# Modulation products in four column groups of TensorE, and another order of the attention units

## What is computed

```python
def trunk_layer(x, mod, lp, rope, ctx_kv):
    sh1, sc1, g1, sh2, sc2, g2 = jnp.split(mod, 6, axis=-1)   # mod = silu(c) @ w_mod + b_mod
    h = layer_norm(x) * (1.0 + sc1) + sh1
    mix, own_kv = token_mixer(h, lp, rope, ctx_kv)
    ...

def diff_attention(q, k, v, lam):          # 4 heads, two maps of 64 each, values of 128
    s = jnp.einsum('bqhmd,bkhmd->bhmqk', qb, k) * scale
    a = jax.nn.softmax(s, axis=-1)
    w = a[:, :, 0] - lam * a[:, :, 1]
    return jnp.einsum('bhqk,bkhd->bqhd', w, v)

def gqa_attention(q, k, v):                # 8 heads of 64, taken two at a time
    s = jnp.einsum('bqhgd,bkhd->bhgqk', qb, k) * scale
    return jnp.einsum('bhgqk,bkhd->bqhgd', jax.nn.softmax(s, axis=-1), v)
```

## Time and profile before

| what | value |
|---|---|
| median of 3 runs | 5316.12 us (5314.84 to 5319.43) |
| the profiled execution | 5326.6 us, its span 5324.8 us |
| mean granted clock of TensorE | 0.898 of full speed |
| PE busy | 4320.0 us, 81% of the span |
| DVE busy | 3689.9 us, 69% |
| ACT, POOL busy | 1406.7 us (26%), 2141.4 us (40%) |

### The profile page before, as it was taken

How to read it: one execution, slowest core, us unless ns; L and a number is a source line. 1 busy time by engine, 2 the same in 40 slices (tenths; PEclk the granted TensorE clock), 3 DMA queues, 4 the chain that set the end, 5 groups by cost and what they waited for, 6 DMA issues and landing times.

```text
span 5324.8 us, 65913 instructions
## 1 busy us (share of the span) xinstructions
PE 4320.0 (81%) x23486; PEld 3688.6 (69%) x23486; DVE 3689.9 (69%) x5666; ACT 1406.7 (26%) x1999; POOL 2141.4 (40%) x1267
## 2 busy tenths in 40 slices
PE   7988799714479999999889888997144799999996
PEld 5855688513369888988778556894133798889885
DVE  2323323689979999999951333236999799999998
ACT  3233311111133332332232332112011333233331
POOL 2200000003368877887621000000133687778874
PEclk9988899857689999999999789998576899999998
DMA  4111111202279999999831211111022899999996
GB/s 169 69 48 66 64 72 72 72 16 71 63 262 404 394 368 366 401 400 362 326 130 55 79 63 52 72 72 71 0 81 85 305 406 385 365 377 402 394 367 241
DMA packets 326651, 1074.16 MB, mean 202 GB/s; under 512 B 25344, under 2 KB 123696, under 8 KB 275824
## 3 DMA queue, kind: packets, MB, share of 16 engines
q0 software_dynamic: 151168, 552.73, 27.3%
q1 hardware_dynamic: 75536, 464.03, 22.4%
q10 hardware_dynamic: 99808, 55.58, 3.6%
HBM read 1012.72 MB, written 59.51 MB: 201 GB/s over the span
## 4 chain that ended last, share of the span: by engine, by line
PE 36%; DVE 31%; POOL 11%; issue 9%; DVEq 8%; ACT 3%; DMA 2%; ACTq 0%; SPq 0%; POOLq 0%
PE PS L547 13%; POOL got L522 10%; DVE acc L1745 9%; PE PS L556 6%; PE PS L557 6%; PE PS L558 6%; DVEq L1746 5%; DVE ring_lo L1719 5%; DVE ohE L1694 3%; PE PS L551 2%; DVE ohA L1694 1%; DVE wtmp L1726 1%; ACT hT L987 1%; DVE got L1742 1%; ACT prob L1110 1%
## 5 line engine op out<-in xcount | busy, mean ns | idle before, releaser
L522 POOL DMA_INDIRECT got<-v_rows,sidx x512 | 878.6, 1716 | 281.4 <-DVE acc L1745 187.8
L522 POOL DMA_INDIRECT got<-u_rows,sidx x512 | 889.0, 1736 | 223.1 <-issue 144.3
L503 POOL TENSOR_TENSOR ohB<-ohE,idxT 128x512 f32<-128x512 f32 x192 | 254.1, 1323 | 1571.8 <-DVE ohE L1694 1571.8
L1265 ACT CAST ring_hi<-ring 128x2048 fp32r<-128x2048 f32 x256 | 489.2, 1912 | 1237.4 <-DMA ring<-weights 1237.4
L556 PE MATMUL PS<-hT_hi,ring_hi 128*128 128x384 f32 x2048 | 688.1, 336 | 55.2 <-DVE ring_lo L1719 55.2
L558 PE MATMUL PS<-hT_hi,ring_lo 128*128 128x384 f32 x2048 | 687.9, 336 | 0.0
L557 PE MATMUL PS<-hT_lo,ring_hi 128*128 128x384 f32 x2048 | 687.2, 336 | 0.0
L556 PE MATMUL PS<-ring_hi,W_hi 128*128 128x512 f32 x1536 | 611.3, 398 | 90.5 <-DVE W_lo L1732 90.5
L1745 DVE SCALAR_TENSOR_TENSOR acc<-got,weight,acc 128x1024 f32<-128x1024 f32 x512 | 657.9, 1285 | 37.1 <-issue 13.2
L1742 DVE SCALAR_TENSOR_TENSOR got<-got,hT 128x1024 f32<-128x1024 f32 x512 | 604.7, 1221 | 27.9 <-issue 16.7
L1719 DVE TENSOR_TENSOR ring_lo<-ring,ring_hi 128x2048 fp32r<-128x2048 f32 x256 | 586.5, 2292 | 29.8 <-issue 29.5
(11 more groups left out here) (251 smaller groups left out, 7912.2 us busy)
## 6 DMA issues: line engine op xcount, KB each, us to landing
ring<-weights SPq DMA_DIRECT2D x392, 1024.0 KB, 7.7
gate_matrix<-stg ACTq DMA_DIRECT2D x12, 4096.0 KB, 15.9
G<-gate_matrix SPq DMA_DIRECT2D x128, 384.0 KB, 9.4
got<-u_rows,sidx POOLq DMA_INDIRECT x512, 8.9
got<-v_rows,sidx POOLq DMA_INDIRECT x512, 8.3
x_wait<-x POOLq DMA_DIRECT2D x2, 2560.0 KB, 24.5
x_mix<-x_wait ACTq DMA_DIRECT2D x2, 2560.0 KB, 9.5
lnr<-lnrows POOLq DMA_DIRECT2D x4, 1024.0 KB, 5.0
```

Source lines behind the costliest of these rows:

```text
L503: nc.gpsimd.tensor_tensor(ohB[:, u % 2, :, :], ohE[:, u % 2, :, :], g, ALU.mult).then_inc(oh_ready, 1)
L522: pool.indirect_dma_start(out=got[:, n % GB, :], out_offset=None, in_=u_rows[:, :] if phase % 2 == 0 else v_rows[:, :], in_offset=bass.Ind ...
L1265: nc.scalar.copy(ring_hi[:, s, :], ring[:, s, :]).then_inc(hi_ready, 1)
```

## The change

Three edits:

1. `cnds` is padded to 32 columns (30 of them zero, by a memset on DVE and a new semaphore `cond_clear`). Product c of a slot goes to column group c % 4 of the array, and its result to PSUM rows 32(c % 4) to 32(c % 4)+31, so a group adds up two products, not eight. The four partial sums are added in `mod_columns`, whose contraction is now over all 128 rows, with a 0/1 selector (`C_SEL`, two more columns of `const`) in place of the identity. ACT's copies to `mrow` have 128 rows, not 2.
2. In attention PE issues scores two units ahead (behind the modulation, scores(1), and then scores(u+2) in unit u: ahead of the transposes for u < 4, behind values(u-1) for u = 4 and 5). ACT runs exps(u+1) ahead of probs_out(u). DVE runs maxima(u+1) ahead of weights_of(u).
3. To make room, the fifth transposed piece of map 0 moves from the unit's own score bank to bank 7, beside the results of values. ACT copies the fifth piece first, and values(u-1) on PE waits for the fifth piece of unit u (`fifth_ready`), since it writes the same bank.

```diff
-        cnds, o = at("cnds", [KC, 2], o)
+        cnds, o = at("cnds", [KC, 32], o)
...
-            return (bank(6), bank(b, 0, P)) if m == 0 else (bank(b + 2), bank(b + 1, 0, P))
+            return (bank(6), bank(7, 0, P)) if m == 0 else (bank(b + 2), bank(b + 1, 0, P))
...
-                    group(out, [(cnds[:, c, :], w[:, c, :]) for c in range(KC)]).then_inc(mod_full, 1)
+                    for c in range(KC):
+                        g = c % 4
+                        last = mm(out[32 * g:32 * g + 32, :], cnds[:, c, :], w[:, c, :], start=(c < 4), stop=(c >= 4))
+                    last.then_inc(mod_full, 1)
...
-                        last = mm(out[:, 2 * k:2 * k + 2], mrow[0:2, k * P:k * P + P], ident[0:2, 0:2],
+                        last = mm(out[:, 2 * k:2 * k + 2], mrow[:, k * P:k * P + P], const[:, C_SEL:C_SEL + 2],
...
-                    modulation(MOD1 + k, PS[0:2, 256 * k:256 * k + 256])
+                    modulation(MOD1 + k, PS[:, 256 * k:256 * k + 256])
...
                             pe.wait_ge(p_ready, base + u - 1)
-                            pe.wait_ge(pT_ready, base_t + turn_group(u - 2, 0 if u < 6 else 1) + 1)
+                            if u >= 6:
+                                pe.wait_ge(pT_ready, base_t + turn_group(u - 2, 1) + 1)
...
                             pe.wait_ge(o_ready, base + u)
+                        if nk == 5:
+                            pe.wait_ge(fifth_ready, (l * (NT - 1) + t - 1) * UNITS + min(u + 2, UNITS))
...
+                    scores(1)
                     for u in range(UNITS):
-                        if u + 1 < UNITS:
-                            scores(u + 1)
+                        if u < 4:
+                            scores(u + 2)
                         for m in range(1 if u < 4 else 2):
                             turn_probs(u, m)
                         if u >= 1:
                             values(u - 1)
+                        if 4 <= u < UNITS - 2:
+                            scores(u + 2)
                     values(UNITS - 1)
...
-                            nc.scalar.copy(pT[:, u % 2, m, 0:4, :].rearrange("p k n -> p (k n)"), four)
-                            nc.scalar.copy(pT[:, u % 2, m, 4, :], fifth).then_inc(pT_ready, 1)
+                            last = nc.scalar.copy(pT[:, u % 2, m, 4, :], fifth)
+                            if m == 0:
+                                last.then_inc(fifth_ready, 1)
+                            nc.scalar.copy(pT[:, u % 2, m, 0:4, :].rearrange("p k n -> p (k n)"), four).then_inc(pT_ready, 1)
...
                     for u in range(UNITS):
+                        if u + 1 < UNITS:
+                            exps(u + 1)
                         for m in range(1 if u < 4 else 2):
                             probs_out(u, m)
-                        if u + 1 < UNITS:
-                            exps(u + 1)
...
                     for u in range(UNITS):
-                        weights_of(u)
                         if u + 1 < UNITS:
                             maxima(u + 1)
+                        weights_of(u)
                         if u >= 1:
                             outputs(u - 1)
```

More of the change, by code:

```diff
@@ L96 @@
 N_GATHER = PHASES * P
-C_ID, C_IOTA, C_COS, C_SIN, C_NSIN, C_ROPEC, C_ROPES, C_ONE, C_LAM, C_BASE = 0, 128, 256, 384, 512, 640, 768, 896, 1024, 1028
-NCONST = 1030
+C_ID, C_IOTA, C_COS, C_SIN, C_NSIN, C_ROPEC, C_ROPES, C_ONE, C_LAM, C_BASE, C_SEL = 0, 128, 256, 384, 512, 640, 768, 896, 1024, 1028, 1030
+NCONST = 1032
 def layer_at(l, per_layer, n):
@@ L193, in trunk @@
         mtmp, t = at("mtmp", [T], t)
-        otmp, t = at("otmp", [2, 256], t)
         oall, _ = at("oall", [NT, D], z_at)
@@ L200, in trunk @@
         lnr, t = at("lnr", [2, D], t)
+        otmp, t = at("otmp", [2, 256], t)
         assert t <= f_at
@@ L275, in trunk @@
         kv_stored = sem("kv_stored")
+        cond_clear = sem("cond_clear")
         cond_ready = sem("cond_ready")
@@ L306, in trunk @@
         t_full = sem("t_full")
+        fifth_ready = sem("fifth_ready")
         pT_ready = sem("pT_ready")
@@ L747, in attend @@
                         for k in range(4):
-                            modulation(MOD2 + k, PS[0:2, 1536 + 256 * k:1792 + 256 * k], t - 1)
+                            modulation(MOD2 + k, PS[:, 1536 + 256 * k:1792 + 256 * k], t - 1)
                         mod_columns(l * N_COL + t + 2, bank(6, 0, 16))
+                    scores(1)
                     for u in range(UNITS):
-                        if u + 1 < UNITS:
-                            scores(u + 1)
+                        if u < 4:
+                            scores(u + 2)
                         for m in range(1 if u < 4 else 2):
@@ L967, in _ @@
             act.wait_ge(setup, 48)
-            A(cnds[:, :, :], cnd[:, :, :], ACT.Silu).then_inc(cond_ready, 1)
+            act.wait_ge(cond_clear, 1)
+            A(cnds[:, :, 0:2], cnd[:, :, :], ACT.Silu).then_inc(cond_ready, 1)
             used = lamw[:, 11:12]
@@ L995, in mod_rows @@
                         act.wait_ge(col_full, n)
-                    nc.scalar.copy(mrow[0:2, :], src).then_inc(mrow_ready, 1)
+                    nc.scalar.copy(mrow[:, :], src).then_inc(mrow_ready, 1)
                 for n in range(2):
-                    mod_rows(layer_at(l, N_MOD, 4 * n + 4), layer_at(l, N_COL, n) if n else None, PS[0:2, 1024 * n:1024 * n + 1024])
+                    mod_rows(layer_at(l, N_MOD, 4 * n + 4), layer_at(l, N_COL, n) if n else None, PS[:, 1024 * n:1024 * n + 1024])
                 root(0, NT)
@@ L1121, in probs_out @@
                         else:
-                            nc.scalar.copy(pT[:, u % 2, m, 0:4, :].rearrange("p k n -> p (k n)"), four)
-                            nc.scalar.copy(pT[:, u % 2, m, 4, :], fifth).then_inc(pT_ready, 1)
+                            last = nc.scalar.copy(pT[:, u % 2, m, 4, :], fifth)
+                            if m == 0:
+                                last.then_inc(fifth_ready, 1)
+                            nc.scalar.copy(pT[:, u % 2, m, 0:4, :].rearrange("p k n -> p (k n)"), four).then_inc(pT_ready, 1)
                     exps(0)
                     if nk == 5:
-                        mod_rows(l * N_MOD + 8 + t * 4, l * N_COL + t + 1, PS[0:2, 1536:2560])
+                        mod_rows(l * N_MOD + 8 + t * 4, l * N_COL + t + 1, PS[:, 1536:2560])
                     for u in range(UNITS):
+                        if u + 1 < UNITS:
+                            exps(u + 1)
                         for m in range(1 if u < 4 else 2):
                             probs_out(u, m)
-                        if u + 1 < UNITS:
-                            exps(u + 1)
                     act.wait_ge(o_full, base + UNITS)
@@ L1320, in _ @@
             reduce = nc.vector.tensor_reduce
+            nc.vector.memset(cnds[:, :, :], 0.0).then_inc(cond_clear, 1)
             dve.wait_ge(setup, 48)
@@ L1835, in constants @@
     base = [layer * EXPERTS for layer in range(LAYERS)]
+    sel = np.eye(32)[:, 0:2]
     parts = [np.eye(P), np.tile(n, (P, 1)), cos, sin, -sin, rc, rs, np.ones((P, P)), np.tile(lam, (P, 1)),
-             np.tile(base, (P, 1))]
+             np.tile(base, (P, 1)), np.tile(sel, (4, 1))]
     table = np.concatenate(parts, 1).astype(np.float32)
```

## The result

The changed kernel takes **5410.09 us** (median of 4 runs, 5407.46 to 5414.65); the kernel before, on the same chip, 5317.77 (4 runs, 5314.84 to 5321.00). The ratio is 1.0174, with a 95% interval of 1.0157 to 1.0192: slower by 1.7%, where +0.9% was forecast: 92 us more, which lies outside the 20 to 75 us of the main forecast, though inside the range of 5315 to 5430. The profiled execution took 5409.75 with a span of 5407.9. Of the 83.1 us that the span grew (5324.8 to 5407.9), attention, from tile 0's copy to `qcur` to the end of the last outputs, has 43.6 in layer 0 (286.8 to 330.3) and 39.7 in layer 1 (286.7 to 326.4).

What follows compares the result with a forecast made beforehand. Modulation alone on PE's path, then a DVE-ACT ring (units 0 to 3) and PE (from unit 4) were taken as bounds. 8 x (-10.5 + 10.3 + 6) = +46, +4, -3: +47, giving 5363 us (+0.9%), range 5315 to 5430.

Steps and rivals of the forecast that it cites:

- the main forecast: Whole kernel: slower by 20 to 75 us (5336 to 5391), given a 50% chance.
- Modulation, -10.5 a tile: Modulation matmuls in each tile: four column groups overlap fully, 15.09 us becomes 4.6, saving 10.5.
- The rival of partial overlap: Modulation: column groups overlap only in part, weight loads stand between matmuls, +45, 5408; none, 5447; 17%, 5 for none.
- The ring of units 1 to 3: Attention: DVE's in-order queue waits for values(u-1) behind turn(u); step 6.7 us at full clock, 8.3 at half, against 5.43.
- The steps at full clock, 55.7 for the stretch: Tile from mod_columns' start to values(7)'s end, all at full clock: 55.7 us against 45.4 before, so +10.3.
- half of the 12: Attention from scores(1): 12 us more a tile if wholly at half clock; half taken, +6, bounds 0 and 12.
- 0.67: Attention: extra us at half clock for one unit's values, the alternative to 1.04 in the 12 us sum.
- The starts: Eight first modulation slots: layer 0's last product shrinks, -3; layer 1 waits for DVE's variance anyway, 0.
- Tile 0, +2 a layer: Tile 0's attention, one key tile: gains the wait for turn and values, loses exponentials; +4 in all (0 to 8).
- the correction from the profiled execution to the median: Whole kernel: the runs' median is 10.5 us below the profiled execution, so 5373.6 becomes 5363.
- PE keeps 2.4 GHz: Attention units: clock stays full, +6 becomes +0, total 5315, or 5296 if steps are shorter; 20%, half of it faster.
- Half clock throughout: Attention and modulation all at half clock: +6 and +2.3 more a tile, +66, 5429; 13%.

## Why the prediction came out as it did

- **Modulation, -10.5 a tile.** Right: -11.2 in tile 1 (15.09 to 3.91), -10.7 on the mean of the eight tiles. The rival of partial overlap falls: the four groups share all 128 rows here, and the weight loads, 1.95 us busy, lie within 3.91 us of matmuls. The rule of the Trainium skill (page "TensorE: Matmul & The Clock Gate", Part 3, The mechanism) that a weight load overlaps matmuls only where the row group differs does not fit this row, and the measurement decides.
- **The ring of units 1 to 3, 6.7 us at full clock, 8.3 at half.** Right, and shown: 6.77 and 6.74 where the clock was 1.00, 8.51 and 8.42 in the changed kernel, with DVE waiting 4.0 to 4.6 us for values as named. What the prediction did not see is that the outputs' place decides, and that putting the maxima back is no help while ScalarE's new order stays: the run with VectorE's old order was slower still, the one with outputs two units behind faster than before.
- **The steps at full clock, 55.7 for the stretch.** Nearly right: 11.2 us were forecast to turn 1 (11.5 measured, in the changed kernel), 44.5 from there on, and the run with the pauses filled took 46.1, of which the added work itself and the clock's fall at the end made 1.9. That leaves 44.2: -0.3 to this term, and +0.3 to the start.
- **The clock: this is the step that failed.** "The new steps are between the two [...] so I take half of the 12: +6." From turn 1 on alone the half clock cost some 10.4 us in tile 1, by the estimate above. The mechanism was named and the term mis-sized: 61.7 were forecast for the stretch and 66.1 measured, and the 4.4 between 6 and 10.4 are that difference, eight times. Both factors of the +6 were too small. The share first: the mean clock of 0.65 from turn 1 on means half clock for 0.7 of the time, not for half; 0.7 of the 12 would be 8.4. Then the 12 itself: the price of "0.67" for the products with values of two maps came from the 3.01 us of the earlier trace rows, which began at full clock and ended at half. Rows 5 has 1.00 up to 387.9, and behind it the kernel before shows:

```profile
387.90:390.70 2.80, 1.35 (x7) 1.16 (x6) 0.47 (x2) 1.04 (x1) 0.00 (x0) 0.50 0.00 0
```

  Wholly at half clock the same products take 4.50 us (the changed kernel's values(4) at 378.95, in the stretch from 377.7 to 391.4 at 0.50), 2.1 more than at full. The share was mis-sized by the comparison of busy shares in the earlier trace rows. At half clock the same work fills more of a stretch: units 1 to 3 show PE busy 13.61 of 17.10 us at 0.50, a higher share than the 12.90 of 18.34 at 1.00 with the added products. A share read at one clock says little about the other.
- **The starts.** Forecast -3 and 0; attention begins 0.4 us later in layer 0 and 2.9 us later behind the experts in layer 1. The products did shrink, but each now waits for its load, and the two mod_columns behind them take 3.58 each where they took 1.94 before. First a row of the kernel before, then rows of the changed kernel's layer 0 and a product of layer 1's start:

```profile
51.37 1.94 PE L570 MATMUL PS<-const,mrow 2*128 2x2 f32 x16
```

```profile
45.84 1.94 PE L568 MATMUL PS<-ring,cnds 128*32 128x256 f32 x16 [2.36 <-DMA ring<-weights]
47.70 3.58 PE L575 MATMUL PS<-const,mrow 128*128 128x2 f32 x16
...
2706.72 1.07 PE L568 MATMUL PS<-ring,cnds 128*32 128x256 f32 x16 [0.27 <-DMA ring<-weights]
```

  So mod_columns gave back twice 1.6 us: I had shrunk the products and left what follows them at its old duration. Layer 1's 2.9 are not explained: from the first product of its modulation to attention the changed kernel takes 281.2 us and the kernel before 278.3, and the nine other kernels here with the column groups take 276.7 to 280.5, the one with these alone 276.7.
- **Tile 0, +2 a layer.** +1.4 each, right.
- **The sum.** Of the 47 us between 5363 and 5410, the tiles have 34 (10.06 each on the mean, where 5.8 was forecast), the starts 6, tile 0 -1, and stages that the change does not touch -3. The other 11 are the correction from the profiled execution to the median: that of before lay above its median, that of the changed kernel (5409.75) does not.
- **The rivals.** "PE keeps 2.4 GHz" did not happen, though the run with filled pauses shows what it would have been worth. "Half clock throughout" (5429) was nearer than the forecast, but not by its mechanism alone: the clock was at half for 0.7 of the time from turn 1 on, and tile 1's modulation, which that rival puts at half clock too, ran at 0.93.

## What to carry to other kernels

Before moving a step ahead in one engine's queue, write down the ring that each in-order wait closes, and count what lies between that wait and the next one: here the new order with outputs one unit behind cost some 20 us a tile, and with outputs two units behind and the old order from unit 4 on it made the fastest kernel. The lengthened ring was paid twice here, in the wait and in the clock (6.77 us a step at 1.00 with the pause filled, 8.51 without), so price a lengthened ring with the rows at 0.50 too, and take the prices from rows that lie wholly at one level. When an edit bundles a sure gain with a reordering, time them apart: here one was -1.5% and the other +3.2%.

## What was not expected of the hardware

- Adding work made the kernel faster: with four more products (1.99 us together) in front of each turn of units 1 to 7 the time fell from 1.0174 to 1.0053 of before, and the granted clock rose from 0.66 to 0.92 over tile 1's stretch.
- Four column groups with all 128 rows each ran fully beside one another: 15.09 to 3.91 us at a clock of 0.92 and 0.93, a factor of 3.86, weight loads included.
- Between 20 and 56 us the windows give a granted clock of 1.00 in both kernels, yet the changed kernel's products take 1.93 us there and 1.07 at the start of layer 1, and mod_columns 3.58 there and 1.95 in tile 1: at the start of this span the durations, not the column, tell the clock.
